# Half-size products, stick-breaking attention and the warm-up of a five-block network: five edits in the order and the number format of work

## The chip, the cores and the metric

The kernel runs on one core of a Trainium2 chip. The time is the device's, in microseconds, from start to end of one execution. The kernel before has a median of 3037.29 us over 3 runs (3037.09 to 3037.88).

## The reference

A sequence of 512 tokens of width 1024 goes through a first block (an S5 state-space mixer and a chunked attention side by side, then a gated feed-forward of width 2816) and four further layers. Layers 0 and 3 mix by stick-breaking attention, layer 1 by differential attention, layer 2 by a short convolution; each layer has a memory attention beside its mixer and a gated feed-forward behind it. Cut to what the change touches:

```python
# stick-breaking attention, 8 heads of 128, one query tile i of 128 rows at a time
z = q[i] @ k[:end].T                               # scores
u = where(mask, softplus(z), 0)
a = where(mask, exp(z - reverse_cumsum(u)), 0)     # the "sticks"
out = a @ v[:end]

# memory: one RMS norm, used by all four layers
mem_n = mem * rsqrt(mean(mem * mem, -1) + 1e-6) * g_mem

# feed-forward
gu = rmsnorm(x) @ w_ffn_in
x = x + (silu(gu[..., :2816]) * gu[..., 2816:]) @ w_ffn_out
```

All inputs and results are float32.

## The kernel before

The activations stay on the chip; all weights are streamed once. Most matmuls are done in the rounded format fp32r in three passes: each operand is split in a high part (a copy rounded to fp32r) and a low part (the exact value minus the high part), and the products high by high, high by low and low by high are added in PSUM (`three`; lines 2245 to 2247 for plain products, line 2610 for half-size ones). A few matmuls are left in full float32.

**Weights.** SyncE issues one load for each unit of 128 x 2048 floats (line 474) into one of two slots of `raw`. Each load waits for the low part that was made last from the slot (`lo_made`). ScalarE makes the high part (`high`, line 752), VectorE the low part (`low`, line 1338), TensorE then uses both.

**The program of each engine** is written out by hand, in order; engines wait for each other by counters. Nothing is reordered at run time: an instruction behind a waiting one waits too.

**Gate and up products.** A gate unit or up unit in the feed-forwards is not multiplied plainly but cut into halves in both directions and done by seven products of half size, of 12 matmuls each (4 contraction tiles x 3 passes, 256 columns, line 2610). The function `seven(s, u0, gc, i, j)` does that on all engines for turn `i` and `j` = 0 (gate) or 1 (up). TensorE's order in it is A11, S1, then the last corner A22 of the unit before, then S2, A12, S4, S3. A corner is a quarter of the weights; an S form is a sum of corners, which VectorE makes from `raw` (lines 1444, 1447, 1450), ScalarE rounds (the high form) and VectorE subtracts (the low form: `corner_low` 1411, `odd_low` 1417 for two odd corners at once, `sums_low` 1423, `sum_low` 1428). Where a partial product is needed in two results, ScalarE copies it from PSUM: three snapshots (lines 844, 851 and 859, the last two to `us`). VectorE adds two of them into the banks of the unit (`take_late`, line 1464, the "late sum"); only then may TensorE start the A22 of that unit. When A22 is done, `finish` (line 1472 or 1474) takes the result out of PSUM and frees the banks for the next turn but one.

In the first turn of a stage (`i` = 0, `j` = 0) there is no unit before; the program does S1's and A22's low parts inside it as well. At its end VectorE does `odd_low`, then `sums_low`; the late sum of this first unit is the first thing that `seven(.., 0, 1)` does. On ScalarE the third snapshot stands behind the high copy of S1. There are five gate/up stages (one in the first block, four in the layers); their first half-size products start at 271.1, 927.9, 1533.9, 2091.7 and 2697.1 us. Eleven gate/up pairs make a stage.

**Feed-forward's second half.** The down products use a ring of two slots for the activations (`ringh`, `ringl`); `down_lows` makes the low parts of unit and ring (line 1517) for a range of down units. In the first block's feed-forward, the norm of the memory is done in between: ScalarE takes a root, VectorE waits for it (line 1955), scales the memory tokens, and then goes on with the low parts of down unit 7.

**Stick heads.** A table of slots (`KZ`, `KTURN`, `KPV`) says behind which column tile of the plain products each step of a head is done. For a head: TensorE does the scores (`KZ`, line 2827 for float32 rows, 2247's helper for the others) into one PSUM area of 1280 columns; ScalarE takes sigmoids; VectorE scans (line 2040 is its last step); TensorE transposes the sticks into the same PSUM area (`KTURN`, line 2812); ScalarE copies all 1280 columns to `sticks_t` (line 1233); TensorE multiplies them with the values (`KPV`, line 2804, eight records in float32 for four key tiles with 512, 384, 256 and 128 query columns). The scores of the next head need that PSUM area free. Score rows i = 2 and 3 are done by `three`, rows 0 and 1 in float32. `qk_lo` (line 2022) makes the low parts of queries and keys.

**Start.** TensorE warms up with 12 and later 22 transposes of the identity (line 2317); between them it transposes x. ScalarE loads its table of functions at its first activation (the wait for `gain_ready` stands ahead of it); line 951 makes the high part of the first half unit, line 1643 the low part. POOL (GpSimd) sets up constants, with a counter for each kind of constant (`angle_ready`, `bl_zero`, `cl_zero`, `st_zero`, `a1_corner`, `t_zero`); the parameters' exponential is line 957 on ScalarE.

Of the kernel before, what the change touches and what calls it, by code (L numbers as in the profile page):

```python
# [140 lines left out]
def build(nc, A, out, ext_dram):  # L141
    with ExitStack() as ctx:
# [284 lines left out]
        sticks_t = at("sticks_t", TMP + 10272, [P, ZW])  # L427
# [176 lines left out]
        def _(pool):  # L604
# [17 lines left out]
            g.memset(er[:, :, 0:1], 1.0).then_inc(S("angle_ready"), 1)  # L622
            g.memset(ei[:, :, 0:1], 0.0).then_inc(S("angle_ready"), 1)
# [46 lines left out]
            g.tensor_scalar(er[:, :, 1:2].rearrange("p i c -> p (i c)"), pr(15), -1.0, 1.0, ALU.mult, ALU.add).then_inc(S("angle_ready"), 1)  # L670
            g.tensor_scalar(ei[:, :, 1:2].rearrange("p i c -> p (i c)"), pr(14), 1.0, None, ALU.mult).then_inc(S("angle_ready"), 1)
# [3 lines left out]
            for j in range(8):  # L675
                g.memset(zero[:, 512 * j:512 * j + 512], 0.0).then_inc(S("bl_zero"), 1)
# [39 lines left out]
            for j in range(10):  # L716
                g.memset(zero[:, 512 * j:512 * j + 512], 0.0).then_inc(S("cl_zero"), 1)
# [4 lines left out]
            for n in range(4):  # L722
                if n >= 2:
                    pool.wait_ge(S("ssm_t"), 14 * (n - 2) + 8)
                g.tensor_copy(rho[n % 2][:, :, :], bcl(rho4[:, 4 * n:4 * n + 4], NC)).then_inc(S("rho_step"), 1)
                pool.wait_ge(S("rho_step"), n + 1)
                g.memset(rho[n % 2][:, :, 0:1], 0.0).then_inc(S("rho_ready"), 1)
                if n == 1:
                    for r in range(2):
                        pool.wait_ge(unit_used, 7)  # L730
                        g.memset(st[r][:, :, :, 0:1], 0.0).then_inc(S("st_zero"), 1)
                    pool.wait_ge(acc_free, 6)
                    pool.wait_ge(S("const_r"), 2)
                    for b in bsb:
                        g.memset(b[0:64, 448:512], NEG).then_inc(S("a1_corner"), 1)
                    pool.wait_ge(S("a1_corner"), 2)
                    pool.wait_ge(S("k_mm"), 1)
                    for s in range(1, 4):
                        g.memset(tm[32 * (3 - s):32 * (3 - s) + 32, :, 0:32 * s], 0.0).then_inc(S("t_zero"), 1)
                    pool.wait_ge(S("t_zero"), 3)  # L740
# [3 lines left out]
        def _(act):  # L744
# [87 lines left out]
            def seven(s, u0, gc, i, j):  # L832
# [25 lines left out]
                done(3)  # L858
                a.activation(us[:, 0, 0:HALF], bank(BBANK[j], HALF), ACT.Copy).then_inc(snap_taken, 1)
# [81 lines left out]

            act.wait_ge(S("gain_ready"), 1)
# [270 lines left out]
            def stick_slot(idx, s):  # L1213
                for h in at_slot(KQK, s):
                    n, l = NH2 * idx + h, 3 * idx
                    act.wait_ge(acc_free, g_in(l) + evicted(2 + 3 * (h // 2), h % 2))
                    if n:
                        act.wait_ge(S("k_z"), n)
                    for m, b in enumerate((qp, kp)):
                        a.activation(qk_hi[:, m, :], b[h // 2 % 2][:, h % 2, :], ACT.Copy).then_inc(S("qk_hi"), 1)  # L1220
                for h in at_slot(KZ, s):
# [6 lines left out]
                for h in at_slot(KTURN, s):  # L1228
# [4 lines left out]
                    a.activation(sticks_t[:, :], ps[:, 0:ZW], ACT.Copy).then_inc(S("k_at"), 1)  # L1233
# [84 lines left out]
        def _(dve):  # L1318
# [157 lines left out]
            def seven(s, u0, gc, i, j):  # L1476
# [6 lines left out]
                if not first:  # L1483
                    take_late(i, g, 120 * s + 6 * j, 60 * s + 3 * j)
# [208 lines left out]
            def input_matrix():  # L1693

                dve.wait_ge(S("bl_zero"), 8)
# [112 lines left out]
            for u in range(8):  # L1808
# [16 lines left out]
                if u == 0:  # L1825
                    dve.wait_ge(S("angle_ready"), 4)
# [11 lines left out]
                if u == 4:  # L1838
                    dve.wait_ge(S("cols_ready"), 8)
                    dve.wait_ge(S("cl_zero"), 10)  # L1840
# [10 lines left out]
                if u >= 6:  # L1851
# [6 lines left out]
                    dve.wait_ge(S("st_zero"), 2)  # L1858
# [6 lines left out]
            for h in range(NH1):  # L1865
                dve.wait_ge(S("a1_z"), h + 1)
                dve.wait_ge(S(f"bias{h % 2}"), 32 * (h // 2 + 1))
                dve.wait_ge(S("a1_corner"), 2)
# [84 lines left out]
            down_lows(0, U_GU1, range(2, 7))  # L1953
# [10 lines left out]
            def second_half():  # L1964
# [6 lines left out]
                     before={0: lambda: down_lows(0, U_GU1, (7,)), 4: second_half}, amid={5: lambda: low(U_DN1 + 13)}, flush=(3,))  # L1971
# [44 lines left out]
            def stick_slot(idx, m0, s):  # L2016
# [24 lines left out]
                for h in at_slot(KPV, s, 2):  # L2041
                    mix_low(h, bank(3), m0 + 2 + h)

# [196 lines left out]
        def _(pe):  # L2240
# [162 lines left out]
            warm(22)  # L2403
# [50 lines left out]
            def outputs(n):  # L2454
# [5 lines left out]
                pe.wait_ge(S("t_zero"), 3)  # L2460
# [335 lines left out]
            def stick_slot(l, s):  # L2796
                base, m0 = NH2 * (l // 3), 8 + 10 * l
                for h in at_slot(KPV, s):
                    pe.wait_ge(S("k_at"), base + h + 1)
# [3 lines left out]
                    for j in range(4):  # L2803
                        e = mm(bank(3, T - P * j, P * j), vp[h // 2 % 2][:, j, P * (h % 2):P * (h % 2) + P],  # L2804
                               sticks_t[:, ZK[j]:ZK[j] + wk(j)], start=j == 0, stop=j == 3, skip_group_check=True)
# [8 lines left out]
                for h in at_slot(KZ, s):  # L2814
                    if h:
                        pe.wait_ge(S("k_at"), base + h)
# [5 lines left out]
                    for i in (0, 2, 3, 1):  # L2822
                        dst, rows = ps[:, ZQ[i]:ZQ[i] + wq(i)], slice(P * i, P * i + P)
                        if i > 1:
                            three(dst, qk_hi[:, 0, rows], qk_lo[:, 0, rows], qk_hi[:, 1, 0:wq(i)], qk_lo[:, 1, 0:wq(i)], i != 2, True)
# [181 lines left out]
```

## Time and profile before

| | |
|---|---|
| median of 3 runs | 3037.29 us (3037.09 to 3037.88) |
| the profiled execution | 3038.19 us |
| its span, first to last instruction | 3036.5 us |
| TensorE (PE) busy | 3000.4 us, 99% |
| TensorE's weight loads (PEld) | 2662.0 us, 88% |
| VectorE (DVE) busy | 2127.7 us, 70% |
| ScalarE (ACT) busy | 1427.4 us, 47% |
| GpSimd (POOL) busy | 51.4 us, 2% |
| HBM | 283 MB, 93 GB/s on average |

Times in the rows are microseconds from the start of the span, unless marked as nanoseconds. TensorE's weight loads run beside its matmuls. The ends of matmuls are modelled, so a single matmul's duration in a timeline is longer than the distance to the next; distances between starts, and the pieces of the chain of waits, give the pace. In brackets behind an instruction stands the idle time of its engine before it, and what ended it. PEclk is the granted TensorE clock as a share of 2.4 GHz.

### The profile page before, as it was taken

How to read it: one execution, taken by the hardware profiler on the slowest of the kernel's cores; microseconds unless marked ns; L12 is line 12 of the kernel's file. 1: busy time of each engine (PE TensorE's matmuls, PEld its weight loads, DVE VectorE, ACT ScalarE, POOL GpSimd, SP SyncE). 2: the span in 40 equal slices, each digit the busy share in tenths (PEclk: the TensorE clock that was granted, in tenths of full speed). 3: DMA queues.
4: the chain of work that ended last, by engine and by line, in shares of the span. 5: the costliest groups of instructions: out<-in, count | busy, mean ns of one | idle time of the engine just before them, and what ended most of it. 6: DMA issues, size and time to landing. Idle time of an engine off the chain costs nothing.

```text
span 3036.5 us, 46958 instructions
## 1 busy us (share of the span) xinstructions
PE 3000.4 (99%) x18453; PEld 2662.0 (88%) x18453; DVE 2127.7 (70%) x2513; ACT 1427.4 (47%) x1957; POOL 51.4 (2%) x148
## 2 busy tenths in 40 slices
PE   9999999999999999999999999999999999999998
PEld 8878998888889998888899988788998888889987
DVE  6988886566558886566588864657886557578864
ACT  3476553444335554334455543325553443355544
POOL 5100000000000000000000000000000000000000
PEclk9999999999999999999999999999999999999999
DMA  5113332342122232311233232223323222133322
GB/s 179 52 53 99 108 115 100 100 143 70 48 92 98 97 104 100 101 56 60 94 98 108 99 104 91 89 70 105 111 97 104 90 84 65 61 109 99 111 90 77
DMA packets 250545, 283.24 MB, mean 93 GB/s; under 512 B 11874, under 2 KB 216864, under 8 KB 250408
## 3 DMA queue, kind: packets, MB, share of 16 engines
q1 hardware_dynamic: 250408, 281.30, 28.5%
q8 instruction: 100, 1.64, 0.2%
q14 instruction: 37, 0.30, 0.0%
HBM read 279.16 MB, written 4.73 MB: 93 GB/s over the span
## 4 chain that ended last, share of the span: by engine, by line
PE 85%; DVE 9%; ACT 3%; issue 2%; POOL 1%; DMA 0%; SPq 0%; DVEq 0%; ACTq 0%
PE ps L2610 31%; PE ps L2245 14%; PE ps L2247 14%; PE ps L2246 14%; PE ps L2890 1%; PE ps L2892 1%; PE ps L2891 1%; PE ps L2804 1%; ACT whi L752 1%; ACT hg L873 1%; DVE wlo L1338 1%; PE ps L2812 1%; PE ps L2871 1%; PE ps L2850 1%; PE ps L2747 1%
## 5 line engine op out<-in xcount | busy, mean ns | idle before, releaser
L752 ACT ACTIVATE whi<-raw 128x2048 fp32r<-128x2048 f32 (+2 forms) x164 | 284.9, 1737 | 657.3 <-PE ps L2247 610.1
L1338 DVE TENSOR_TENSOR wlo<-raw,whi 128x2048 fp32r<-128x2048 f32 (+2 forms) x164 | 339.4, 2070 | 291.5 <-ACT whi L752 291.2
L2610 PE MATMUL ps<-th,wh 128*128 128x256 f32 x1600 | 454.8, 284 | 12.2 <-DVE ps L1464 9.5
L2610 PE MATMUL ps<-tl,wh 128*128 128x256 f32 x1600 | 454.2, 284 | 0.0
L2610 PE MATMUL ps<-th,wl 128*128 128x256 f32 x1600 | 454.2, 284 | 0.0
L2245 PE MATMUL ps<-hh,whi 128*128 128x512 f32 x896 | 359.3, 401 | 0.0
L2247 PE MATMUL ps<-hh,wlo 128*128 128x512 f32 x896 | 349.7, 390 | 0.0
L2246 PE MATMUL ps<-hl,whi 128*128 128x512 f32 x896 | 349.4, 390 | 0.0
L2610 PE MATMUL ps<-hl,wh 128*128 128x256 f32 x1200 | 339.6, 283 | 0.0
L2610 PE MATMUL ps<-hh,wl 128*128 128x256 f32 x1200 | 339.6, 283 | 0.0
L2610 PE MATMUL ps<-hh,wh 128*128 128x256 f32 x1200 | 339.6, 283 | 0.0
L2245 PE MATMUL ps<-ringh,whi 128*128 128x512 f32 x860 | 334.9, 389 | 3.0 <-DVE ringl L1517 3.0
L2246 PE MATMUL ps<-ringl,whi 128*128 128x512 f32 x860 | 334.6, 389 | 0.0
L2247 PE MATMUL ps<-ringh,wlo 128*128 128x512 f32 x860 | 334.6, 389 | 0.0
L2610 PEld LDWEIGHTS ps<-th,wh 128*128 128x128 f32 x1600 | 308.6, 193 | 13.9 <-issue 10.4
L2610 PEld LDWEIGHTS ps<-tl,wh 128*128 128x128 f32 x1600 | 308.6, 193 | 0.2
L2610 PEld LDWEIGHTS ps<-th,wl 128*128 128x128 f32 x1600 | 308.6, 193 | 0.0
L2610 PEld LDWEIGHTS ps<-hl,wh 128*128 128x128 f32 x1200 | 230.4, 192 | 0.2
L2610 PEld LDWEIGHTS ps<-hh,wh 128*128 128x128 f32 x1200 | 230.4, 192 | 0.2
L2610 PEld LDWEIGHTS ps<-hh,wl 128*128 128x128 f32 x1200 | 230.4, 192 | 0.0
L2245 PEld LDWEIGHTS ps<-hh,whi 128*128 128x128 f32 x896 | 168.3, 188 | 39.8 <-issue 4.4
L1417 DVE TENSOR_TENSOR wl<-raw,wh 128x1024 fp32r<-128x1024 f32 x95 | 116.4, 1225 | 122.5 <-ACT wh L820 122.5
(458 smaller groups left out, 6009.7 us busy)
## 6 DMA issues: line engine op xcount, KB each, us to landing
raw<-in_w_ffn_in SPq DMA_DIRECT2D x88, 1024.0 KB, 5.1
raw<-in_w_in SPq DMA_DIRECT2D x59, 1024.0 KB, 5.3
raw<-in_w_ffn_out SPq DMA_DIRECT2D x40, 1024.0 KB, 5.0
raw<-in_w_o SPq DMA_DIRECT2D x32, 640.0 KB, 4.4
raw<-in_w_gate SPq DMA_DIRECT2D x11, 1024.0 KB, 5.4
raw<-in_w_up SPq DMA_DIRECT2D x11, 1024.0 KB, 5.3
raw<-in_w_down SPq DMA_DIRECT2D x10, 1024.0 KB, 5.0
raw<-in_w_mem_kv SPq DMA_DIRECT2D x8, 1024.0 KB, 5.1
```

The lines of the kernel that those rows point to most:

```text
L752: a.activation(whi[:, slot, 0:n], raw[:, slot, 0:n], ACT.Copy).then_inc(hi_made, 1)
L873: a.activation(hg[:, t, :], x[:, t, :], ACT.Identity, scale=col(gain_col(r) + t)).then_inc(ffn_hi, 1)
L1338: v.tensor_tensor(wlo[:, u % 2, 0:n], raw[:, u % 2, 0:n], whi[:, u % 2, 0:n].bitcast(F32), ALU.subtract).then_inc(lo_made, 1)
L1417: v.tensor_tensor(blocks_of_two(wl8[:, q, :]), odd_corners(slot, p), blocks_of_two(wh8[:, q, :]).bitcast(F32), ALU.subtract).then_inc(lo_m ...
L2245: mm(dst, wh, xh, start=first, stop=False, skip_group_check=True)
L2246: mm(dst, wh, xl, start=False, stop=False, skip_group_check=True)
L2247: return mm(dst, wl, xh, start=False, stop=last, skip_group_check=True)
L2610: e = mm(bank(b, HALF), wgt[:, q, w], xx, start=start and k == 0 and m == 0, stop=k == KD // 2 - 1 and m == 2, skip_group_check=True)
L2747: e = mm(bank(b + r, MEM, MEM * i), mq[rows, f, t:t + P], km[rows, l, f, :], start=i == 0, stop=True, skip_group_check=True)
L2804: e = mm(bank(3, T - P * j, P * j), vp[h // 2 % 2][:, j, P * (h % 2):P * (h % 2) + P], sticks_t[:, ZK[j]:ZK[j] + wk(j)], start=j == 0, sto ...
L2812: e = tr(ps[:, o:o + P], stick[:, ZQ[i] + P * j:ZQ[i] + P * j + P], ident[:, :])
L2850: e = mm(bank(6 + d, T - P * j, P * j), vp[hd % 2][:, j, P * d:P * d + P], dpt[:, ZK[j]:ZK[j] + wk(j)], start=j == 0, stop=j == 3, skip_gr ...
```

## The change

1. Gate/up stages, first turn: ScalarE takes the third snapshot ahead of the high copy of S1. VectorE does the late sum of the first unit at the end of `seven(.., 0, 0)`, in front of `sums_low`, and `odd_low` comes last.
2. Start: the table of ScalarE is loaded ahead of its first wait; the second row of warm-up transposes has 12 in place of 22. POOL's six counters become one, `pool_set`, with the counts in order of issue.
3. Memory norm: the low parts of down unit 7 are made ahead of VectorE's wait for the memory's root.
4. Stick heads: score row 1 goes by `three` too. The sticks of key tiles 0 and 1 (columns 0 to 895) are split by ScalarE (`sticks_hi`) and VectorE (`sticks_lo`), likewise the values of these tiles (`v_hi`, `v_lo`, once for a pair of heads, at slot `KPV` - 2), and the value products of these tiles go by `three`. Key tiles 2 and 3 stay in float32, from a copy of 384 columns. Scores and values wait for both parts.

```diff
@@ block.scalar, seven
                 a.activation(us[:, 1, 0:HALF], bank(DBANK[j], HALF), ACT.Copy).then_inc(snap_taken, 1)
+
+                def early():
+                    done(3)
+                    a.activation(us[:, 0, 0:HALF], bank(BBANK[j], HALF), ACT.Copy).then_inc(snap_taken, 1)
+                if first:
+                    early()
                 if not last:
                     summed(4)
                     sum_high("S1", p, form_hi)
...
-                done(3)
-                a.activation(us[:, 0, 0:HALF], bank(BBANK[j], HALF), ACT.Copy).then_inc(snap_taken, 1)
+                if not first:
+                    early()
...
+            a.preload_act_table(ACT.Exp)
             act.wait_ge(S("gain_ready"), 1)
...
+                for h in at_slot(KPV, s, -2):
+                    if h % 2 == 0:
+                        n = NH2 * idx + h
+                        act.wait_ge(acc_free, g_in(3 * idx) + evicted(3 + 3 * (h // 2), 0))
+                        if n:
+                            act.wait_ge(S("k_o"), n)
+                        a.activation(v_hi[:, :, :], vp[h // 2 % 2][:, 0:2, :], ACT.Copy).then_inc(S("v_hi"), 1)
...
-                    a.activation(sticks_t[:, :], ps[:, 0:ZW], ACT.Copy).then_inc(S("k_at"), 1)
+                    a.activation(sticks_t[:, :], ps[:, WIDE:ZW], ACT.Copy).then_inc(S("k_at"), 1)
+                    a.activation(sticks_hi[:, :], ps[:, 0:WIDE], ACT.Copy).then_inc(S("k_at"), 1)
@@ block.vector, seven
-                if not first:
+                if not first and not (j == 1 and isinstance(i, int) and i == 0):
                     take_late(i, g, 120 * s + 6 * j, 60 * s + 3 * j)
...
-                if not last:
+                if first:
+                    take_late(i, 0, 120 * s + 6, 60 * s + 3)
+                    sums_low(p, form(5))
+                    odd_low(p, 1 - slot, 1 - j, form(4))
+                elif not last:
                     odd_low(p, 1 - slot, 1 - j, form(4))
                     sums_low(p, form(5))
@@ block.vector, first block's feed-forward and the memory
-            down_lows(0, U_GU1, range(2, 7))
+            down_lows(0, U_GU1, range(2, 8))
             dve.wait_ge(S("mem_sd"), 1)
...
-                     before={0: lambda: down_lows(0, U_GU1, (7,)), 4: second_half}, amid=...
+                     before={4: second_half}, amid=...
@@ block.vector, stick_slot
+                for h in at_slot(KTURN, s):
+                    dve.wait_ge(S("k_at"), 2 * (NH2 * idx + h) + 2)
+                    v.tensor_tensor(sticks_lo[:, :], ps[:, 0:WIDE], sticks_hi[:, :].bitcast(F32), ALU.subtract).then_inc(S("k_al"), 1)
+                for h in at_slot(KPV, s, -2):
+                    if h % 2 == 0:
+                        dve.wait_ge(S("v_hi"), NH2 // 2 * idx + h // 2 + 1)
+                        v.tensor_tensor(v_lo[:, :, :], vp[h // 2 % 2][:, 0:2, :], v_hi[:, :, :].bitcast(F32), ALU.subtract).then_inc(S("v_lo"), 1)
@@ block.tensor
-            warm(22)
+            warm(12)
...
                 for h in at_slot(KPV, s):
-                    pe.wait_ge(S("k_at"), base + h + 1)
+                    pe.wait_ge(S("k_at"), 2 * (base + h + 1))
+                    pe.wait_ge(S("k_al"), base + h + 1)
+                    pe.wait_ge(S("v_lo"), (base + h) // 2 + 1)
...
+                        if j < 2:
+                            three(dst, v_hi[:, j, c], v_lo[:, j, c], sticks_hi[:, keys], sticks_lo[:, keys], j == 0, False)
+                            continue
...
                 for h in at_slot(KZ, s):
                     if h:
-                        pe.wait_ge(S("k_at"), base + h)
+                        pe.wait_ge(S("k_at"), 2 * (base + h))
+                        pe.wait_ge(S("k_al"), base + h)
...
-                        if i > 1:
-                            three(dst, ...)
+                        if i > 0:
+                            e = three(dst, ...)
```

## Rows read from the trace of the kernel before

**Rows 1.** Who waited for whom, TensorE: us in total, times, longest us

```profile
PE ps L2610 <- DVE ps L1464: 9.5, 5, 2.0
...
PE ps L2610 <- ACT us L859: 2.7, 4, 0.8
```

**Rows 2.** Timeline 0 to 32: start us, us, engine, line, operation, count [idle before <- releaser]

```profile
6.28 1.28 ACT L947 ACT_TABLE_LOAD   x1 [6.28 <-PE ps L2326]
...
9.24 3.54 PE L2317 MATMUL ps<-ident 128*128 128x128 f32 x22
...
10.01 1.23 DVE L1643 TENSOR_TENSOR wlo<-raw,whi 128x1024 fp32r<-128x1024 f32 x1 [0.20 <-ACT whi L951]
...
12.53 0.47 PE L2245 MATMUL ps<-hh,whi 128*128 128x512 f32 x1
```

**Rows 3.** Windows of line 2317: us, busy (count), PEclk, DMA share, GB/s

```profile
9.20:10.20 1.00, 0.96 (x5) 1.00 (x6) 1.00 1.07 372
11.20:12.20 1.00, 1.00 (x11) 1.00 (x10) 1.00 1.03 379
```

**Rows 4.** Chain of waits, 0 to 140: start us, us, engine, line

```profile
16.11 0.23 ACT ssp L957
```

**Rows 5.** Timeline 536 to 549, the memory's norm

```profile
536.42 1.90 ACT L800 ACTIVATE ringh<-actr 128x2048 fp32r<-128x2048 f32 x1
...
542.17 0.17 DVE L1955 RECIPROCAL rec<-rec 128x2 f32<-128x2 f32 x1 [7.29 <-ACT rec L1151]
...
545.91 2.29 DVE L1517 TENSOR_TENSOR ringl<-actr,ringh 128x2048 fp32r<-128x2048 f32 x1
...
548.34 0.47 PE L2245 MATMUL ps<-ringh,whi 128*128 128x512 f32 x1 [2.96 <-DVE ringl L1517]
```

**Rows 6.** Chain of waits, stick heads: 384, 512, 2x256 (float32), 256, value columns

```profile
733.58 0.17 PE ps L2247
...
734.21 0.23 PE ps L2247
734.44 0.43 PE ps L2827 x2
734.88 0.12 PE ps L2890
...
737.74 2.16 PE ps L2804 x8
```

**Rows 7.** Timeline 937 to 952, VectorE and ScalarE, first turn of stage 2

```profile
939.34 1.22 DVE L1417 TENSOR_TENSOR wl<-raw,wh 128x1024 fp32r<-128x1024 f32 x1
939.51 1.06 ACT L823 ACTIVATE wh<-stmp 128x1024 fp32r<-128x1024 f32 x1 [2.67 <-DVE stmp L1450]
...
941.75 0.69 DVE L1464 TENSOR_TENSOR ps<-ps,us 128x512 f32<-128x512 f32 x1
...
943.55 1.23 DVE L1444 TENSOR_TENSOR stmp<-raw 128x1024 f32<-128x1024 f32 x1 [0.51 <-DMA raw<-in_w_ffn_in]
...
947.10 1.22 DVE L1474 TENSOR_TENSOR gs<-ps,rs 128x1024 f32<-128x1024 f32 x1
```

**Rows 8.** Timeline 937 to 952, TensorE

```profile
942.59 0.35 PE L2610 MATMUL ps<-th,wh 128*128 128x256 f32 x1 [2.00 <-DVE ps L1464]
```

**Rows 9.** The page, DMA issues: KB each, us from issue to landing

```profile
raw<-in_w_ffn_in SPq DMA_DIRECT2D x88, 1024.0 KB, 5.1
```

**Rows 10.** Windows of TensorE: us, busy (count), PEclk, DMA share, GB/s

```profile
942.60:951.20 8.60, 8.60 (x59) 0.80 0.40 127
1548.20:1556.80 8.60, 8.60 (x72) 1.00 0.43 133
```

**Rows 11.** Timeline 730 to 733.2, a hand-over between stick heads

```profile
730.29 1.24 ACT L1233 ACTIVATE sticks_t<-ps 128x1280 f32<-128x1280 f32 x1 [5.28 <-PE ps L2812]
...
732.84 0.38 PE L2827 MATMUL ps<-kp,qp 128*128 128x128 f32 x2
...
733.04 0.69 DVE L2178 SCALAR_TENSOR_TENSOR kp<-ps,rs 128x512 f32<-128x512 f32 x1 [2.35 <-PE ps L2247]
```

More of the change, by code:

```diff
@@ L426, in build @@
         stick = at("stick", TMP + 5152, [P, ZW])
-        sticks_t = at("sticks_t", TMP + 10272, [P, ZW])
+        WIDE = ZK[3]
+        sticks_hi = at("sticks_hi", TMP + 10272, [P, WIDE], F32R)
+        sticks_lo = at("sticks_lo", US0, [P, WIDE], F32R)
+        sticks_t = at("sticks_t", TMP + 10272 + 4 * WIDE, [P, ZW - WIDE])
+        v_hi = at("v_hi", SQB0, [P, 2, 256], F32R)
+        v_lo = at("v_lo", SQB0 + 2048, [P, 2, 256], F32R)
         qk_hi, qk_lo = (at(f"qk_{n}", TMP + 15392 + 4096 * k, [P, 2, T], F32R) for k, n in enumerate(("hi", "lo")))
@@ L669, in _ @@
             double_angle(pr(14), pr(15), pr(14), pr(15))
[L670 to L671 removed]
+            g.tensor_scalar(er[:, :, 1:2].rearrange("p i c -> p (i c)"), pr(15), -1.0, 1.0, ALU.mult, ALU.add).then_inc(S("pool_set"), 1)
+            g.tensor_scalar(ei[:, :, 1:2].rearrange("p i c -> p (i c)"), pr(14), 1.0, None, ALU.mult).then_inc(S("pool_set"), 1)
             link(g.tensor_scalar(pr(7), pr(6), -1.0, 1.0, ALU.mult, ALU.add))
@@ L1970, in _ @@
             residual(2, lambda t: down_tile(U_DN1, 6, t), lambda t: bank(t), "add",
-                     before={0: lambda: down_lows(0, U_GU1, (7,)), 4: second_half}, amid={5: lambda: low(U_DN1 + 13)}, flush=(3,))
+                     before={4: second_half}, amid={5: lambda: low(U_DN1 + 13)}, flush=(3,))
             norm(2, after_diag=lambda: low(U_KV + 2))
@@ L2803, in stick_slot @@
                     for j in range(4):
-                        e = mm(bank(3, T - P * j, P * j), vp[h // 2 % 2][:, j, P * (h % 2):P * (h % 2) + P],
-                               sticks_t[:, ZK[j]:ZK[j] + wk(j)], start=j == 0, stop=j == 3, skip_group_check=True)
+                        dst, keys, c = bank(3, T - P * j, P * j), slice(ZK[j], ZK[j] + wk(j)), slice(P * (h % 2), P * (h % 2) + P)
+                        if j < 2:
+                            three(dst, v_hi[:, j, c], v_lo[:, j, c], sticks_hi[:, keys], sticks_lo[:, keys], j == 0, False)
+                            continue
+                        e = mm(dst, vp[h // 2 % 2][:, j, c], sticks_t[:, ZK[j] - WIDE:ZK[j] - WIDE + wk(j)],
+                               start=False, stop=j == 3, skip_group_check=True)
                     e.then_inc(S("k_o"), 1)
@@ L2823, in stick_slot @@
                         dst, rows = ps[:, ZQ[i]:ZQ[i] + wq(i)], slice(P * i, P * i + P)
-                        if i > 1:
-                            three(dst, qk_hi[:, 0, rows], qk_lo[:, 0, rows], qk_hi[:, 1, 0:wq(i)], qk_lo[:, 1, 0:wq(i)], i != 2, True)
+                        if i > 0:
+                            e = three(dst, qk_hi[:, 0, rows], qk_lo[:, 0, rows], qk_hi[:, 1, 0:wq(i)], qk_lo[:, 1, 0:wq(i)], i != 2, True)
                             continue
```

30 lines of the change are left out of this document (15 added, 15 removed).

## Prediction, made before the changed kernel was run

> **What bounds the kernel now.** I read the engines' totals first: TensorE (PE) is busy 99% of the span, so only two things can shorten it: fewer PE cycles, or less PE waiting. Next the view of who waited for whom, for PE: its largest wait is for the late sum of the half-size products (line 1464), 9.5 us in five places of up to 2.0, then 2.7 us in four places for a snapshot copy (line 859) [rows 1]. These stand at the five starts of the gate/up stages. Then the timelines of those places, of the start and of the memory norms; then the chain of waits, whose pieces give the pace of matmuls without the modelled tails.
>
> **Start.** The first real product starts at 12.53, right behind 22 warm-up transposes that began at 9.24; what it needs, the weights' first low half (line 1643), was there at 10.01+1.23 = 11.24 [rows 2]. The transposes start at 5 in one us and at 11 in one us two us later [rows 3]: the clock rose from 1.2 to 2.4 GHz among them. With 0.21 us each before the rise (the pace of 5 in a us at half clock) and 0.109 after, 22 in 3.29 us means 8.6 at half clock; twelve take 8.6x0.21+3.4x0.109 = 2.2 us and end at 11.45. So PE starts at 11.5: -1.0 us. From there the chain runs over the parameters' exponential at 16.11 [rows 4], which stands behind PE's row transposes, through POOL and VectorE to the first attention; all of it moves along, so the 1.0 is kept. Bounds: 0 if a DMA holds the chain, 1.3 if the warm-up were no limit (12.53 against 11.24). The table load, moved ahead of ScalarE's first wait, leaves 1.28 us of ScalarE's time at 6.28 [rows 2]. I take 0 for it: even if the first weights' high half came that much earlier, the twelve transposes end after the low half is ready. Bounds 0 and -0.2, what is left of the wait. The merged counters keep every count in the order of issue on POOL: 0, nothing waits for more than before.
>
> The Trainium skill (TensorE: Matmul & The Clock Gate, What's actually happening) has it that TensorE's clock is gated down by default and activity lifts it. That speaks against taking warm-up work out. The rise falls within the twelve that stay [rows 3], so by the row the sum keeps its -1.0; by the rule, if the rise waited for more, rival 4 below.
>
> **Memory norms.** VectorE stands 7.29 us until 542.17 for the memory's root; only then come scaling, the low weights and the low activations of down unit 7, the latter 545.91 to 548.20, and PE, which waited 2.96 us, goes on at 548.34 [rows 5]. The high parts are complete at 536.42+1.90 = 538.3. With unit 7's low parts ahead of the norm, they take 2.2 us each from 536.5 on, the second from about 538.9 to 541.1, four us before PE wants them. -3.0 us. What follows (scaling 542.4 to 545.1, then the additions) moves up by the same 3 us, so unit 8 keeps its margin of some 0.4 us. Bounds -2.5 (unit 8 late by that margin) and -3.1.
>
> **First turn of the five gate/up stages.** Each product is 12 matmuls at 0.12 us [rows 6], 1.44 us. In the second stage, taken as the pattern: VectorE runs the low halves of the odd corners (939.34, 1.2 us), of the two sums (1.2) and only then the late sum (941.75, 0.69), and PE starts the product behind it at 942.59, 0.15 us after its end; it had waited 2.00 [rows 7, 8]. New: late sum 939.34 to 940.03. The snapshot that it needs is taken before the S1 copy, so PE's 0.8 us wait for line 859 goes too; the product before then ends earlier and PE could take the next at 939.4, but the late sum is ready at 940.2 with its latency: a wait of 0.7. Then PE needs the sums' low halves: ScalarE makes the high ones at 939.51 to 940.57 [rows 7], VectorE the low ones to 941.8, so S2 starts at 942.0 instead of 941.6: 0.4 more. What follows on VectorE doesn't move: line 1444 at 943.55 waits for a weight DMA that was issued behind a low half which keeps its place, and from it the row of six instructions leads to line 1474, 947.10 to 948.32 [rows 7], which frees the bank of the next turn's first product. So PE starts that at 948.5, a wait of 0.7. Before, it was 942.59 + 5x1.44 + 1.5 of clock = 951.3 (below). Without the clock the gain is 1.4 us, not the 2.8 of the two waits: the DMA landing is late next. I take 1.4 for stages 2, 4 and 5, 1.0 for stage 3 (its snapshot wait is the short one of the four) and 1.2 for stage 1 (its wait was 9.5-4x2.0 = 1.5, and it has no snapshot wait): 6.4 us. Bounds: 3 (half is given back at the next turn, where late sum and PE meet within 0.1 us) and 12.2 (all of both waits).
> The odd halves' low parts now come behind the sums', 2.4 us later, and the load of the unit after next waits for them. Issued at 943.1, behind the low part's end at 942.9, it lands after 5.1 us [rows 9] at 948.2 and is wanted by the next turn's line 1444, at about 951.8: hidden, cost 0; without that cover each us late would cost five, one in each stage.
> **Clock.** From 942.60 on PE made 59 matmuls in 8.6 us, from 1548.20 on, after the same wait of 2.0, 72; the granted clock is 0.80 and 1.00 [rows 10]. 13 matmuls of 0.12 are 1.5 us. Two of the five stages show it (the one at 2106 too). The waits that remain are 0.7, 0.4 and 0.7 apart from each other, and in this trace waits of 1.5 us at such a start passed without a fall; so both falls go: -3.0. Bounds 0 and -3.0.
>
> **Stick attention, 16 heads.** Chain pieces: fp32r at 128x512 0.23, 384 0.17 to 0.18, 256 0.12; fp32 at 256 columns 0.43; the eight fp32 value matmuls of a head (1280 columns) 2.16 [rows 6]. Third score row: 0.43 becomes 3x0.12, -0.07. Values of key tiles 0 and 1 (896 of the 1280 columns): 2.16x896/1280 = 1.51 becomes 3x0.227+3x0.175 = 1.21, -0.31. Together 0.38x16 = 6.0 us less on PE, which is the bound there.
> Added on ScalarE: the copy of 1280 columns becomes one of 384 and one of 896, and a copy of 512 for each pair of heads (0.6 us by the same slope, in front of a wait for transposes of more than 5 us, hidden). Added on VectorE: a subtraction of 896 columns from PSUM per head, of 512 (0.69) per pair. PE's next score waits for both. Price of that wait, no row shows the operations: ScalarE's copies take 1.24 for 1280 columns and 1.06 for 1024 [rows 7, 11], 0.7 to 0.8 ns a column, so 0.93 for 896 and 0.52 for 384; successive ones overlap by 0.1. VectorE's of two operands take 0.69 for 512 columns and 1.22 for 1024 [rows 7], so 1.09 for 896. From the end of the transposes (730.26): 0.03+0.42+0.93+0.04+1.09+0.15 = 2.65, so PE could start at 732.9; it now starts at 732.84, and VectorE is idle for 2.35 us until 733.04 in just that place [rows 11]. In other heads the distance is 2.6 to 2.7. Six hand-overs a layer are so tight (the others have 3 us and more): 12 x 0 to 0.07, I take 0.3 in all. Bounds 0 and 12x0.6 = 7.2 (one VectorE instruction of 0.7 in front of it each time). So -5.7, bounds -6.0 and +1.2. The extra 0.7 us of the pair's subtraction delays the eviction of 733.04 by 0.4; behind it VectorE waits for ScalarE anyway.
> The Trainium skill (ScalarE: Activation LUTs, What ACT_TABLE_LOAD costs) prices a plain activation at 186 ns + 0.833 per column, overlapping by 93: an estimate from it is 1.35 us for the two copies, as from the rows.
>
> **Sum.** 1.0+3.0+6.4+3.0+5.7 = 19.1 us off the profiled execution's 3038.19 (span 3036.5), 3019.1. The runs shown have a median of 3037.29, 0.9 lower; from there 3018.2. I forecast 3018.5.
>
> **Rivals.**
> 1. All waits of the two kinds go without a remainder (12.2 and the clock), start 1.3: the DMA landing wouldn't bind. For it: the idle times themselves. Against: line 1444 has its DMA wait in the rows. 6 us better: 3012. Chance 0.15.
> 2. The hand-over in the stick heads costs as much as the matmuls save (0.4 to 0.5 each of 12, because the high copy waits or the PSUM reads are slower than line 2022's kind): 3024. For it: no margin at all. Against: VectorE idle there. 0.17.
> 3. The clock falls stay, since the waits remain in pieces near each other: 3.0 back, 3021.5. 0.12.
> 4. The rise comes behind the twelve transposes, so that the first real products run at half pace: by the price of a fall [rows 10] 1.5 us back, 3020. For it: the pause between the warm-up's end and the first product is then new. Against: the rise came 2.0 us after the first transpose, and twelve last 2.2. 0.06. The Trainium skill's section named above points this way.
> 5. Slower: the subtraction for the next score queues behind the 2.3 us weight subtraction (line 1338) on VectorE, so each of the 12 tight hand-overs waits 2.3 us, and the clock falls at half of them (6x1.5). 27.6+9-19 = +17: 3055. It decides once the weight's low part stands ahead of sticks_lo in VectorE's order; it turns slower than before at 1.6 us per hand-over. Against: in the program's order that weight part comes after slot 23's work. 0.02.
> 6. The reordering does nothing because the DMA wait swallows all: 3025 to 3028. 0.05.
> The forecast itself: 0.43, own range 3015 to 3022.
> Range for 8 in 10: 3012 to 3028, from rivals 1 to 6 without the slow one; the middle of the hand-over's bounds (half of 7.2 above the forecast's sum, with rival 3 beside it) sets the upper end. A change below 0.2% (6 us) is about what can't be told from none. Faster 0.95, same 0.03 (rivals 2 and 3 together with a hand-over near its bound), slower 0.02.
>
> **What would show it.** First real product near 11.5 and the exponential near 15.1. No wait for line 1517's ring at unit 7. At each gate/up start three waits of PE of 0.4 to 0.7 us in place of 0.8 and 2.0, the next turn's first product 20.5 us after the stage's first (stages 2 to 5), and no granted clock below 1 there. In the stick heads 1.21 us for six fp32r value matmuls, waits for sticks_lo of at most 0.1 us. I am wrong if PE's waits for sticks_lo add up to over 3 us, or if the gate/up starts keep a single wait of about 2 us.

## The result: 20 us less, and the profile after

The changed kernel has a median of 3017.55 us (6 runs, 3016.9 to 3018.84), the kernel before, run beside it, 3037.68 us: a ratio of 0.9933, 95% interval 0.9923 to 0.9944. That is 20.1 us less where 19.1 were forecast. The profiled execution took 3016.93 us, 21.3 less than that of before.

Who waited for whom, TensorE, in the changed kernel (us in total, times, longest; line 2641 is line 2610 of before, 1484 is 1464, 1494 is 1474, 1667 is 1643, 1896 is 1872, 2540 is 2509, 2357 is 2326):

```profile
PE ps L2641 <- DVE gs L1494: 2.6, 5, 0.6
...
PE ps L2540 <- DVE mx L1896: 2.5, 4, 1.6
...
PE ps L2641 <- DVE ps L1484: 1.9, 4, 0.6
...
PE ps L2357 <- DMA xtok<-in_x: 1.5, 1, 1.5
PE ps L2276 <- DVE wlo L1667: 1.4, 1, 1.4
```

The late sum holds TensorE for 1.9 us in place of 9.5 [rows 1], the snapshot for nothing, and a wait for the freed bank (line 1494) is new. The next three fences are from stage 2. VectorE, timeline:

```profile
927.73 0.69 DVE L1470 TENSOR_TENSOR stmp<-raw,stmp 128x512 f32<-128x512 f32 x1
928.34 0.69 DVE L1484 TENSOR_TENSOR ps<-ps,us 128x512 f32<-128x512 f32 x1
929.60 1.23 DVE L1443 TENSOR_TENSOR wl<-stmp,wh 128x1024 fp32r<-128x1024 f32 x1 [0.57 <-ACT wh L828]
930.75 1.22 DVE L1437 TENSOR_TENSOR wl<-raw,wh 128x1024 fp32r<-128x1024 f32 x1
...
936.22 1.21 DVE L1494 TENSOR_TENSOR gs<-ps,rs 128x1024 f32<-128x1024 f32 x1
```

TensorE's waits in the same stretch:

```profile
929.17 0.36 PE L2641 MATMUL ps<-th,wh 128*128 128x256 f32 x1 [0.58 <-DVE ps L1484]
937.49 0.39 PE L2641 MATMUL ps<-hh,wh 128*128 128x256 f32 x1 [0.59 <-DVE gs L1494]
```

And the windows of the same length as in [rows 10] (us, busy and count, granted clock, DMA share, GB/s):

```profile
929.10:937.70 8.60, 7.89 (x61) 1.00 0.67 231
1532.00:1540.60 8.60, 7.96 (x62) 1.00 0.70 229
```

The late sum stands 0.57 us of idle ahead of the sums' low halves: VectorE makes it while ScalarE rounds the sums. The clock is 1.00 in both. At the memory's norm, VectorE has unit 7's low part done before it waits:

```profile
533.48 2.28 DVE L1541 TENSOR_TENSOR ringl<-actr,ringh 128x2048 fp32r<-128x2048 f32 x1
536.90 0.17 DVE L1979 RECIPROCAL rec<-rec 128x2 f32<-128x2 f32 x1 [1.14 <-ACT rec L1163]
```

VectorE's idle time there fell from 7.29 us [rows 5] to 1.14, and no wait of TensorE stands behind it. A hand-over between stick heads:

```profile
721.80 0.49 ACT L1252 ACTIVATE sticks_t<-ps 128x384 f32<-128x384 f32 x1 [4.76 <-PE ps L2849]
722.19 0.91 ACT L1253 ACTIVATE sticks_hi<-ps 128x896 fp32r<-128x896 f32 x1
723.13 1.09 DVE L2069 TENSOR_TENSOR sticks_lo<-ps,sticks_hi 128x896 fp32r<-128x896 f32 x1 [0.94 <-ACT sticks_hi L1253]
...
724.44 0.46 PE L2865 MATMUL ps<-kp,qp 128*128 128x128 f32 x2
...
729.18 0.40 PE L2276 MATMUL ps<-sticks_hi,v_hi 128*128 128x512 f32 x1
...
730.40 0.81 PE L2841 MATMUL ps<-sticks_t,vp 128*128 128x256 f32 x4
```

The low part ends at 724.22 and the scores start 0.22 later, where I had counted 0.15. The six rounded value matmuls take 1.22 us, from 729.18 to 730.40 (1.21 forecast). The start:

```profile
0.81 1.28 ACT L953 ACT_TABLE_LOAD   x1 [0.81 <-PEq L3034]
...
9.03 1.47 PE L2348 MATMUL ps<-ident 128*128 128x128 f32 x12
9.52 1.06 ACT L963 ACTIVATE whi<-raw 128x1024 fp32r<-128x1024 f32 x1 [1.97 <-DMA raw<-in_w_in]
...
11.90 0.50 PE L2276 MATMUL ps<-hh,whi 128*128 128x512 f32 x1 [1.40 <-DVE wlo L1667]
```

The twelve transposes take 1.47 us, not 2.2: the clock had risen at 6.1 us in this execution, where transposes go from 0.21 to 0.11 us apart, and not at 11.2 as in that of before. TensorE now waits 1.40 us for the first half unit, which the DMA brought at 9.5.

Milestones of several profiles, us (a stage's turn is the distance from its first product to the next turn's first product; a stick layer goes from its first transpose to the start of the next gate/up stage):

| | before | again | after | again |
|---|---|---|---|---|
| first product | 12.53 | 11.86 | 11.90 | 11.69 |
| start of stage 1 | 271.12 | 268.82 | 267.06 | 267.24 |
| turn of stages 1, 2, 3 | 20.45, 23.41, 21.53 | 20.46, 23.42, 21.55 | 19.09, 20.57, 20.16 | 19.12, 20.58, 20.18 |
| turn of stages 4, 5 | 23.41, 21.93 | 23.43, 21.93 | 20.57, 20.57 | 20.57, 20.57 |
| end of stage 1 to first stick transpose | 251.88 | 253.48 | 248.65 | 248.66 |
| stick layers | 198.97, 198.96 | 198.96, 198.98 | 196.47, 196.47 | 196.45, 196.48 |

### The profile page after: what moved, and what is told of

Same layout as the page of the kernel before. It is cut to its first block, busy times and chain, and to the rows that moved or that the text cites. A ratio compares the mean times of both kernels' runs of the same rounds, so it can differ in the third digit from the quotient of the medians.

```text
span 3015.2 us, 47109 instructions
## 1 busy us (share of the span) xinstructions
PE 2987.0 (99%) x18491; PEld 2658.5 (88%) x18491; DVE 2147.9 (71%) x2537; ACT 1431.6 (47%) x1981; POOL 50.7 (2%) x148
## 3 DMA queue, kind: packets, MB, share of 16 engines
q8 instruction: 100, 1.64, 0.2%
## 4 chain that ended last, share of the span: by engine, by line
PE 84%; DVE 10%; ACT 3%; issue 2%; POOL 1%; DMA 0%; SPq 0%; DVEq 0%; ACTq 0%
PE ps L2641 30%; PE ps L2276 15%; PE ps L2278 14%; PE ps L2277 14%; PE ps L2928 1%; PE ps L2929 1%; PE ps L2930 1%; ACT hg L884 1%; ACT whi L757 1%; DVE wlo L1358 1%; PE ps L2849 1%; DVE stmp L1464 1%; PE ps L2909 1%; PE ps L2888 1%; PE ps L2778 1%
## 5 line engine op out<-in xcount | busy, mean ns | idle before, releaser
L2278 PEld LDWEIGHTS ps<-hh,wlo 128*128 128x128 f32 x896 | 168.2, 188 | 35.9
```

Source lines behind the costliest of these rows:

```text
L2278: return mm(dst, wl, xh, start=False, stop=last, skip_group_check=True)
```

## Experiments

**The kernel before, unchanged (before_again).**

> The kernel before, unchanged, profiled once more. Theory A (a fall of TensorE's clock is brought about by the kernel's own waits): the granted clock falls at the same three places again (137.5, 943 and 2107 us), and the first half-size product of stage 1 comes at 271.1 within 0.2 us. Theory B (whether a wait brings a fall is partly chance): at least one of the three is missing or a new one is there, and the spans differ by 1.5 us or 2.7 us for each. If B holds, part of the 20.1 us measured is not the change's.

3037.39 us (one run). Windows of TensorE:

```profile
546.40:549.80 3.40, 3.40 (x10) 0.50 0.55 212
549.80:553.20 3.40, 3.40 (x16) 1.00 0.00 0
942.30:945.70 3.40, 3.40 (x18) 0.50 0.86 273
2106.30:2109.70 3.40, 3.40 (x18) 0.50 0.77 244
```

Theory B holds, with a part of A: the falls at 137, 943 and 2107 us are there again (each 0.7 or 0.8 us earlier), a fourth is new (546, behind the 2.96 us wait at the memory's norm), and stage 1 began 2.3 us earlier than in the first profile of the same program. So neither the start nor the falls are the same from one execution to the next.

**The first turns alone (turns_only), and each engine's half of that edit.** ScalarE's half and VectorE's half, from the diff of the change:

```diff
# snapshot_only
+                if first:
+                    early()                       # third snapshot ahead of S1's high copy
# late_sum_only
+                    take_late(i, 0, 120 * s + 6, 60 * s + 3)
+                    sums_low(p, form(5))
+                    odd_low(p, 1 - slot, 1 - j, form(4))
# turns_only: both
```

> Before with the reordered first turn of the five gate/up stages alone. My theory: the next turn's first product comes 20.6 us after the stage's first in stages 2, 4 and 5, 20.2 in stage 3, 19.1 in stage 1, the same places as in the full change; 9.8 us less in the profiles if both falls of the clock in these turns are gone, of which 6.9 without them. Rival: part of it needs the other edits (the clock's state from the stick heads before), then the turns are later by up to 1.5 us each and the gain is 5 us or less. Time 3027.9 by the first, 3032 or more by the rival.

> Before with VectorE's part of the first-turn edit alone: the late sum ahead of the sums' low parts, these ahead of the odd ones; ScalarE's third snapshot stays behind the S1 copy. My theory: VectorE's row of instructions decides the turn, the 0.8 us wait for the snapshot lies inside the wait for the late sum. So the next turn's first product comes 20.6 us after the stage's first in stages 2, 4 and 5, as with both edits; A22 starts at 12.5 (12.25 with both). Rival: the two waits add up (9.5 and 2.7 us in the profile of before), and leaving the snapshot where it was costs 0.8 us in each of four stages: 21.3 to 21.4.

> Before with ScalarE's part of the first-turn edit alone (third snapshot ahead of the S1 copy). My theory: nothing is gained, PE reaches the late sum 0.8 to 0.9 us sooner and waits 2.8 to 2.9 us there in place of 2.0; A22 starts at 14.67 and the next turn's first product comes at 21.9 (23.4 with a fall of the clock), as before. Rival: 0.8 us less in four stages (A22 at 13.8).

turns_only had a median of 3026.41 us (before 3037.11; ratio 0.9966, 0.9954 to 0.9979). Its turns came at 19.09, 20.60, 20.20, 20.59 and 20.59, within 0.04 us of those with all edits, so nothing in them leans on the rest. TensorE's waits in its stage 2:

```profile
939.50 0.36 PE L2620 MATMUL ps<-th,wh 128*128 128x256 f32 x1 [0.61 <-DVE ps L1470]
947.83 0.39 PE L2620 MATMUL ps<-hh,wh 128*128 128x256 f32 x1 [0.59 <-DVE gs L1480]
```

late_sum_only (one run, 3027.16 us) gave 20.58 in stages 2, 4 and 5, though the wait for the snapshot was as large as before:

```profile
933.21 0.35 PE L2614 MATMUL ps<-th,wh 128*128 128x256 f32 x1 [0.78 <-ACT us L859]
945.66 0.39 PE L2614 MATMUL ps<-hh,wh 128*128 128x256 f32 x1 [0.60 <-DVE gs L1474]
```

snapshot_only (one run, 3038.81 us) gained nothing; the time just moved into the wait for the late sum:

```profile
PE ps L2616 <- DVE ps L1470: 13.1, 5, 3.0
```

13.1 is 9.5 + 2.7 [rows 1] and 0.9 more. Behind the longer wait of 3.0 us the clock fell in stage 5 too (turn 23.23, before 21.93). The rival, that the two waits are worth their sum, is refuted: the snapshot's wait was worth nothing, and its half of the edit brought 0.0 us of turn.

**The order at the memory's norm alone (norm_order_only).**

```diff
-            down_lows(0, U_GU1, range(2, 7))
+            down_lows(0, U_GU1, range(2, 8))
```

> Before with the low parts of down unit 7 ahead of the memory's norm alone. My theory: 2.96 us of PE's wait go, unit 8's low part is still in time, and 3.1 to 3.2 us are gained at the first stick head; the fall of the clock behind that wait (at 546 us, in three of four profiles that have the wait) goes with it, up to 1.5 us more. Rival: unit 8 is late and a wait of 0.5 us or more comes up there, gain under 2.7 us. Time 3034.

3030.92 us (before 3037.19; ratio 0.9984, 0.9974 to 0.9994). From the end of stage 1 to the first stick transpose it took 248.67 us, 3.21 less than in the first profile of before and 4.81 less than in the second, which had the fall at 546. No wait at unit 8. Of the seven profiles with the old order four had that fall, of the seven with the new order none. The medians differ by 6.3 us, more than this step and that fall give (I had expected 3034): six of the ten executions took 3029.1 to 3031.4 us, four 3034.0 to 3035.5. The profiled one is of the first group; by chance it had no fall at 137 and none in stage 2 (turn 21.93) though the wait of 2.0 was there, and the usual one in stage 4. Windows of TensorE at these two waits:

```profile
935.40:938.80 3.40, 3.21 (x27) 1.00 1.03 332
2098.20:2101.60 3.40, 3.40 (x19) 0.50 0.85 275
```

**Stick values and score row, with the one counter (sticks_counter).** The new waits need the counters that the six old ones of POOL leave free, so the edit alone (sticks_only) gave no kernel and no result, and both go in together.

> Before with the rounded stick values and score row and the one POOL counter (the new counters need the room that the six old ones leave). My theory: matmuls save 0.35 us a head, hand-overs give back 0.3 us a layer, 5.0 us in all, 2.5 in each of the two layers. Rival: the saving of the full change leans on the other edits, and is under 4 us here with waits above 0.2 us at the first score matmuls. Time 3032.

3031.56 us (before 3037.19, 3032 expected; ratio 0.9983, 0.9973 to 0.9992). The two stick layers took 196.46 and 196.45 us, 2.51 less each, the same as in the full change. The rival is refuted.

**The start alone (start_only), and the changed kernel with 22 transposes (start_22).**

> Before with the start edits alone (12 warm-up transposes, table load first, one POOL counter). The full change's trace has stage 1 start 4.1 us earlier: 0.6 at the first product, 0.7 by the POOL chain between 30 and 52 us, 2.7 by a fall of the clock at 137.5 us that is missing. My theory: the first two come from the start edits and repeat (1.4 us), the fall is a matter of chance and may be there or not. Rival: the fall is gone because of the start's timing, and the gain is 4.1 us again. Time 3036.3 against 3033.6.

> The changed kernel with 22 warm-up transposes again. My theory: the first product waits for the first half unit's low part (1.4 us in the changed kernel's profile), and 10 transposes at full clock (1.1 us) fit into that; they cost something only where the clock rises as late as 11 us, as it did in some profiles of before. First product at 11.9 within 0.2 if the clock rises before 8 us, at 12.5 to 12.8 if it rises after 11. Rival: it is the warm-up's end that sets the start, 12.5 in both cases.

start_only: 3035.78 us (before 3037.11; ratio 0.9996, 0.9986 to 1.0006), no difference that can be told. Its first product came at 11.73, stage 1 at 268.43, with a fall at 137 half as long as before's. start_22: 3018.0 us (one run), clock up at 5.2, first product at 11.48, earlier than the 11.9 that I expected, since the half unit came at 9.1. Its first product's row:

```profile
11.48 0.50 PE L2276 MATMUL ps<-hh,whi 128*128 128x512 f32 x1 [0.39 <-DVE wlo L1667]
```

The ten more transposes shrink the wait from 1.4 to 0.39 us and hold up nothing. Where the clock rises late they do; turns_only, with the old start, shows that:

```profile
9.66 3.42 PE L2327 MATMUL ps<-ident 128*128 128x128 f32 x22
10.48 1.23 DVE L1653 TENSOR_TENSOR wlo<-raw,whi 128x1024 fp32r<-128x1024 f32 x1 [0.67 <-ACT whi L957]
...
12.83 0.47 PE L2255 MATMUL ps<-hh,whi 128*128 128x512 f32 x1
```

**The changed kernel, unchanged (after_again).**

> The changed kernel, unchanged. My theory: what the edits bring is fixed (turns, norm, sticks repeat within 0.1 us); what the start brings is mostly not the edits' but chance, since kernels with the old start put stage 1 anywhere between 267.3 and 271.1 us. So stage 1 starts between 266.5 and 269.5 here, and the falls at the gate/up starts and at 546 stay away. Rival: the start edits fix it, and stage 1 starts at 267.1 within 0.3 again. Time 3017.5, 20 us (18.5 to 21.5) less than before.

3018.15 us (before 3037.9; ratio 0.9934, 0.9921 to 0.9948). Stage 1 at 267.24, which here speaks for the rival; the other kernels with the new start say otherwise. Over all profiles stage 1 starts at 267.3 to 271.1 with the old start (seven, mean 269.4) and at 266.5 to 268.5 with the new one (six, mean 267.6); the first product at 11.8 to 12.8 (mean 12.4) and at 11.3 to 12.5 (mean 11.8).

**One more instruction in each hand-over (extra_wait).**

```diff
                     dve.wait_ge(S("k_at"), 2 * (NH2 * idx + h) + 2)
+                    v.memset(stick[:, 0:640], 0.0)
```

> The changed kernel with one memset of 640 columns on VectorE in front of every low part of the sticks. My theory: a hand-over has no room, and each of the 12 tight ones puts the memset's whole duration (0.35 to 0.7 us) on TensorE's path: 4 to 8 us more, waits at the first score matmuls of that size, none at the four others. Rival: the plain products between hide half of it, 2 us or less. If the clock falls behind any of these waits, 1.5 us for each fall on top.

3023.82 us (one run). VectorE and TensorE at the same hand-over:

```profile
722.73 0.59 DVE L2069 MEMSET stick<- 128x640 f32 x1 [1.10 <-ACT sticks_hi L1253]
723.23 1.03 DVE L2070 TENSOR_TENSOR sticks_lo<-ps,sticks_hi 128x896 fp32r<-128x896 f32 x1
...
724.47 0.46 PE L2866 MATMUL ps<-kp,qp 128*128 128x128 f32 x2 [0.54 <-issue]
```

Each stick layer took 3.61 us more, 0.60 for each of its six tight hand-overs, which is the memset's 0.59; 0.30 to 0.54 of each shows as a wait. There is no room at all. The clock did not fall behind any of these twelve waits. (The wait is put down to "issue": the profile did not see its releaser.)

**Two further edits (further), and the one of them that holds (sticks_pieces).**

```diff
# further only: VectorE, second half of the first turn
+                    if early_finish:               # i == 0 and j == 1
+                        finish(s, i, g)
                     summed(5)
                     sum_s4(p, 1 - slot)
# both: ScalarE, then VectorE
-                    a.activation(sticks_t[:, :], ...)       # 384 columns
                     a.activation(sticks_hi[:, :], ...)      # 896 columns
+                    a.activation(sticks_t[:, :], ...)
...
+                    dve.wait_ge(S("k_at"), 2 * (NH2 * idx + h) + 1)
+                    v.tensor_tensor(sticks_lo[:, 0:T], ps[:, 0:T], sticks_hi[:, 0:T], ...)
                     dve.wait_ge(S("k_at"), 2 * (NH2 * idx + h) + 2)
+                    v.tensor_tensor(sticks_lo[:, T:WIDE], ps[:, T:WIDE], sticks_hi[:, T:WIDE], ...)
```

> The changed kernel with two more edits: in the second half of the first turn VectorE takes the first unit's result out of PSUM ahead of the S4 sum, not behind it; and in the stick heads the wide high copy comes first and its low part is made in two pieces (512 columns at once, 384 behind the narrow copy). My theory: the wait for the freed bank is 0.59 us at each of the five stages and goes, the turn comes 20.0 us after the stage's start in place of 20.6 (19.6 in stage 3, 18.7 to 19.1 in stage 1); in the heads the low part ends 0.2 us sooner and the hand-over costs nothing: 2.5 to 3.0 and 0.4 to 0.6, 3.2 us less than the changed kernel. Rival: the S4 sum is what comes late next, its high and low parts hold up the next turn's S2, and under 1 us is gained.

> The changed kernel with the low part of the sticks in two pieces behind the wide copy alone, without the moved bank release. In the kernel that had both, a stick layer took 195.96 us from its first transpose to the next gate/up stage in place of 196.47, and a gate/up stage's turn came 0.6 us sooner but the stage ended 0.15 us (0.54 in stage 3) later against its start. My theory: these two are independent, so here both layers keep their 0.5 us and the five stages are as in the changed kernel (20.57 for the turn in stages 2, 4, 5; 206.2 us in all): 1.0 us less than the changed kernel at equal starts and clocks, 3016.5 to 3017.5. Rival: the loss in the stages came from the pieces, not from the release; then stages 2, 4 and 5 take 206.3 again.

further: 3018.01 us (before 3037.9; ratio 0.9935, 0.9922 to 0.9949), no better than the changed kernel beside it (3018.15). The turns came 0.6 us earlier as meant (19.98 in stages 2, 4 and 5), and the stages were 0.15 us longer as a whole, stage 3 by 0.54 (for that one see the next run). TensorE's waits in its stage 2 tell why:

```profile
930.30 0.36 PE L2649 MATMUL ps<-th,wh 128*128 128x256 f32 x1 [0.59 <-DVE ps L1484]
941.64 0.38 PE L2649 MATMUL ps<-th,wh 128*128 128x256 f32 x1 [0.49 <-DVE ps L1484]
```

The wait for the bank is gone and stands at the next turn's late sum, two products later; the S4 sum, its rounding and its low half were pushed back in front of it. The rival was right for that edit. For the sticks my theory held, 195.95 us a layer, and the pieces brought 1.0 us in both layers where I had expected 0.4 to 0.6.

sticks_pieces: 3017.28 us (before 3037.82; ratio 0.9933, 0.992 to 0.9947), layers of 195.95 and 195.93 us, stage 2 of 206.17 as in the changed kernel, so the pieces cost the stages nothing there. Stage 3 was 0.3 us longer than in the changed kernel (its turn at 20.47, not 20.16), against my expectation. VectorE's timeline of that stage shows it waiting for the weights, which it doesn't do in the changed kernel:

```profile
1535.89 1.22 DVE L1464 TENSOR_TENSOR stmp<-raw 128x1024 f32<-128x1024 f32 x1 [0.38 <-DMA raw<-in_w_ffn_in]
```

The same wait is 0.44 us in extra_wait, which has no pieces (turn at 20.51), and 0.49 in further, so some 0.4 of the 0.54 us there are not the moved release's. Why the load came late in these three profiles stays open. Against the changed kernel's 3017.55 and 3018.15 the times cannot separate 1.0 us, the profiles do. Where the time in the sticks came from is in the chain of waits, first of the changed kernel, then of this one (start us, us, engine, line):

```profile
724.27 0.23 PE ps L2278
724.50 0.40 PE ps L2865 x2
```

```profile
724.88 0.23 PE ps L2280
725.11 0.22 PE ps L2867 x2
```

The first score row is the same two records; 0.40 in the one is 0.22 of work and 0.18 of waiting that no row calls a wait.

## Why the prediction was right, step by step

The changed kernel's profile against that of before:

| step | forecast | measured |
|---|---|---|
| start, first product | -1.0 | -0.64 |
| between first product and stage 1 | 0 | -3.4 |
| memory norm | -3.0 | -3.2 |
| first turns without clock | -6.4 | -6.8 |
| falls in the first turns | -3.0 | -2.9 |
| stick matmuls | -6.0 | -6.0 |
| stick hand-overs | +0.3 | +1.0 |
| rest | 0 | +0.7 |
| sum | -19.1 | -21.3 |

- **First turns: right in mechanism and size.** I expected waits of 0.7, 0.4 and 0.7 and the next turn at 20.5; the starts of the products in stage 2 give 0.7, 0.3 (with 0.1 behind it) and 0.7, and 20.57. The five turns gained 1.36, 2.84, 1.37, 2.84 and 1.36, 9.8 in all; two falls of 1.47 are in it. Stage 3 was mis-sized (1.0 expected): I gave it less because its snapshot wait was short, and that wait was worth nothing anywhere. One step was wrong though it did no harm: I had TensorE reach the late sum sooner by the snapshot's move and counted that as part of the gain. In late_sum_only the 0.78 us wait stays and the turn comes at the same time.
- **What binds there was half right.** I named the landing of a weight load. The load landed by 932.40, and the first sums (line 1444 of before, 1464 of after) began at 932.67, right behind VectorE's own work that ended at 932.57: both bind, within 0.2 us. Moving the release ahead of the S4 sum then showed that it is VectorE's row of work that counts, for the next 0.6 us of wait just moved on. Where the load landed later, in stage 3 of three profiles, VectorE waited 0.38 to 0.49 us for it, and in the two of them that keep the release's place the turn came 0.3 us later: there the landing binds, as I had said.
- **The clock in the first turns: right.** The falls in stages 2 and 4 are in five and in six of the six profiles with the old turns, and in none of the 40 turns of the eight profiles with the new ones. Waits of up to 0.8 us there were never followed by a fall. Those of 2.0 were in 9 of 10 cases in stages 2 and 4 and in none of 10 in stages 3 and 5, of the same length; in snapshot_only the three of 3.0 were, and that of 2.6 in stage 3 was not. What decides between these was not found.
- **Memory norm: right** (3.0 against 3.2). I missed that the wait there is also a place where the clock can fall, though not in the profile I had: four of seven profiles, some 0.9 us on average (4/7 of the 1.6 us between 253.48 and 251.88).
- **Sticks: one term mis-sized.** sticks_pieces takes 3.02 us less a layer than before (198.97 - 195.95): 0.38 a head, exactly the sum over the matmuls. The changed kernel keeps 2.5 of it, so the hand-overs cost 0.5 a layer and not 0.15. My sum for a hand-over (2.65 us, found 2.67) was right; wrong was to set it against the start of the first score matmul's record, which comes 0.10 us later than it could where the work behind it comes 0.18 later (at the hand-over shown). In the expectation of the runs I put the matmuls at 0.35, having read starts of records in the place of the chain's pieces; that was wrong too, and it was the experiment that set it right. Rival 5's price is confirmed by extra_wait: one instruction ahead costs its full length.
- **Start: right for one execution, not for all.** I took it that the transposes hold up the first product, from one execution in which the clock rose at 11.2 us. It rose after 10 us in five of the 14 profiles, four of them with 22 transposes, and these hold it up by 0.9 to 1.3 us (turns_only: the half unit's low part ready at 11.7, first product at 12.83). In the other nine it rose between 5.2 and 7.2; then 22 transposes end before the low part too (before_again waits 0.36 us behind them) and taking ten out gives only a longer wait, 1.4. So the edit is worth about 1.1 or nothing, by chance: 0.57 between the means of first products. Even in this profile the -1.0 became -0.64, as the data came later (low part ready at 11.85, before 11.24). Rival 4 came about in none of the six profiles with twelve: even in the one with a late rise (further, at 10.8) the clock was up before the transposes ended, and the first product came at 11.76. The Trainium skill (TensorE: Matmul & The Clock Gate, What's actually happening), by which activity lifts the clock, would let one expect a later rise with fewer transposes; no run here shows that.
- **Between the first product and stage 1: not foreseen.** 2.6 of the 3.4 us are the fall of the clock at 137 us, which the first profile of before had and that of after had not; 0.7 is the chain of POOL and VectorE between 30 and 52 us, which was long in four of the eight profiles with 22 transposes (before, snapshot_only, sticks_counter, start_22) and in none of the six with twelve. Whether the transposes have a part in that stays open. Among the profiles with the old start that fall was long in four, short in one, absent in two; with the new start absent in four, short in two (short in start_22 too). Whether the new start makes it rarer or this is chance stays open. So the 21.3 us between the two profiles flatter the change; the medians' 20.1 are the better number, and the steps that repeat (9.8 for the turns, 3.2 and 0.9 for the norm, 5.0 for the sticks) make 18.9 of it. The remaining 1.2 lie within what the start may bring (start_only: 1.3, with an interval wider than that). The four edits alone took 10.7, 6.3, 5.6 and 1.3 us off the medians, 23.9 in all; each of these has an interval of some 3 us to either side, so the 3.8 us over the 20.1 can't be read as the edits standing in each other's way.
- **How much of it was luck.** That 19.1 came within 1.0 us of 20.1 is in part luck: the norm brought 1.1 us more than I gave it, nearly all of it a fall that I had not seen, the turns 0.4 more, and the sticks 0.7 less; and I booked both falls of the turns as sure, where one of them was missing in one of six profiles.

## What to carry to other kernels

Two waits in a row in front of the same engine need not be worth their sum: here only the last one in the chain was worth anything, and taking away the first alone lengthened the second. Before moving an instruction ahead on a saturated engine, list what it pushes back, for the wait comes out again at the next reader. And profile the unchanged kernel twice before you read a gain out of two profiles: here the same program differed by 2.3 us at one milestone, more than several of the edits bring.

## What the runs showed of the hardware

- A wait of TensorE may stay hidden: 0.18 us were visible only as a first matmul piece of 0.40 in place of 0.22, and no view of waits lists it. Such waits add up to 0.5 us a layer (196.47 against 195.95).
- The granted clock fell to 0.50 (1.2 of 2.4 GHz) behind waits of 1.6 to 3.0 us, and equal waits at equal places did or did not bring a fall from one execution to the next: behind the 1.6 us at 135 to 137 us in 8 of 14 profiles, behind the 1.64 us at 604 to 613 us in none of 14, behind the 1.5 us of stage 1 in none of six.
- At the gate/up starts and the stick heads it never fell behind waits of 0.3 to 0.8 us. At the kernel's end it did: in five of the 14 profiles (after_again, at 3005.7) the fall came 2.7 to 3.1 us behind a wait of 0.78 us, with the last small transposes and one-column matmuls still to be done. The length of a single wait does not decide it.
- The table load of 1.28 us at 0.81 us is wholly hidden; behind it ScalarE's first activation started at 6.29, where before it started at 7.58. The first product did not profit, for the half unit's data came at 9.5.
